# Stick-breaking units spread among the softmax units of block 1's attention, and head squares of block 2 moved to ScalarE

## The chip, the cores and the metric

The kernel runs on one core of one Trainium2 chip. The metric is the device time of one execution in microseconds (us); the time before is the median of three runs, 1567.66 us (1566.31 to 1568.97). Engines: PE is TensorE, ACT is ScalarE, DVE is VectorE, POOL is GpSimd, SP is the queue that loads the weights.

## The reference

Two blocks of two layers each, on 256 tokens of 1024 features, all in float32. Block 1, a layer:

```
h = rmsnorm(x, norm_mix);  proj = h @ w_in            # q, k, v of 24 heads of 64, and 3 x 1024 gate columns
o_a = dilated_mixture(q, k, v)       # 4 slots, each 3 heads of different dilation in one softmax
o_b = moba_attention(q, k, v)        # 6 heads, causal softmax
o_c = stick_breaking_attention(q, k, v)   # 6 heads, no softmax:
    z = q k^T * scale;  log_1m = log_sigmoid(-z) (0 where not causal)
    a = exp(log_sigmoid(z) + exclusive suffix sum of log_1m);  o = a v
merged = gates[0] * (o_a @ w_out_a) + gates[1] * (o_b @ w_out_b) + gates[2] * (o_c @ w_out_c)
x = x + merged @ w_o;  x = x + relu(rmsnorm(x) @ w_up)^2 @ w_down
```

Block 2 takes x and a context of 256 tokens. Each layer projects the modulated norm of both (512 rows), and every query and key head gets an RMS norm of its own:

```
def rms_norm(x, g): return x * rsqrt(mean(x * x, axis=-1) + EPS) * g      # over the 64 features of a head
q = apply_rope(rms_norm(heads(aq, 8), q_norm));  k = apply_rope(rms_norm(heads(ak, 2), k_norm))
```

Layer 0 has a global attention and a Hyena branch, layer 1 a windowed and a neighbourhood attention.

## The kernel before, in words

**Precision and staging.** Every large product is made of three fp32r passes (`product`, L617 to L619): high by high, and the two cross terms. Weights arrive in `raw` by SP, ACT rounds each quarter (128x1024) to `w_high` (L1343), and DVE subtracts it to `w_low` (L1756). There are four slots for split quarters, so a quarter is rounded when the product that used the one four before it has ended. The class `Splits` puts these roundings in ACT's and DVE's streams: `splits.due(key)` issues each rounding whose slot is free by the time PE reaches `key`. `copy_out`, which ACT uses to empty a bank, calls it first.

**Block 1's attention.** `units_of_block1` lists 26 units: 8 of kind A (four slots, two query tiles each), 12 of kind B (six heads, two tiles) and 6 of kind C, one per stick-breaking head. Before, all C stand last, as units 20 to 25. All three engines walk this list in step; for unit u PE runs `scores(u)`, `second(u-1)`, three or four steps of the gates' projection (`advance(filler, ...)`: three for A, four for B and C, a step being the three passes of one k and one tile) and `values(u-2)`. The 96 filler steps are six slabs of 16. The banks of a slab close when PE is in units 5, 9, 13, 17, 21 and 25, and ACT copies the two banks out at the end of the unit in which they close (`copy_gate`, L1447 and L1451, four instructions). In the next units it does a logarithm step (L1458, L1460) and an exponent step (L1466) for each. Three banks serve the gates.

- A softmax unit: scores on PE (L801, L806), mask and maximum on DVE (L1926 to L1942), exponential on ACT (L1379), transposes on PE (L832), copy on ACT (L1350), values on PE (L857), scaled copy on ACT (L1434).
- A C unit: scores on PE (L811, L812), mask on DVE (L1921), three instructions on ACT (L1478, L1480, L1482), then DVE (L1960, L1963: `stick_summed`), the suffix sums on PE (L822 to L824), DVE (L1947), an exponential on ACT (L1417: `stick_weights`), values on PE (L845 to L847), copy on ACT (L1429).

In ACT's stream a unit begins with `take_second(u-1)`, then the roundings that are due, then its exponential or its three C instructions, then `take_values(u-2)`, an exponent step, a logarithm step, and the gate copies. After the last unit PE waits until every `o` bank is empty and transposes the heads' outputs (L881); ACT and DVE split these (L1502, L1979), and the output projection starts (L617).

**Block 2's head norms.** `heads_norm` on DVE waits until ACT has emptied the banks, squares the heads tile by tile (L2098), sums the squares (L2100), and after ACT's Ln and Exp refines and multiplies (L2105 to L2118), with roundings' subtractions in between. PE transposes the normed heads (L1019) and starts the attention. The norms are (layer, j): (0, 0) and (1, 3) of 4 tiles x 8 heads, (0, 1) and (1, 1) of 4 tiles x 2 heads, (1, 0) and (1, 2) of 2 tiles x 8 heads. POOL meanwhile adds masks to the relative biases (L2541), and splits the last weights.

Of the kernel before, what the change touches and what calls it, by code (L numbers as in the profile page):

```python
# [26 lines left out]
ACT = mybir.ActivationFunctionType  # L27
# [115 lines left out]
def units_of_block1():  # L143

    soft = [("A", s, t) for s in range(N_A) for t in range(TILES)]
    soft += [("B", b, t) for b in range(N_B) for t in range(TILES)]
    return soft + [("C", c, 0) for c in range(N_C)]
# [64 lines left out]
def two_blocks(nc, A, C, out):  # L212
    ctx = ExitStack()
    with ctx:
# [61 lines left out]
        work = arena[:, 0:2048]  # L276
        ada_rows = arena[:, 2560:3072]
# [238 lines left out]
        def bank(*key):  # L516
            return banks[number[key][0]]
# [777 lines left out]
        def _(act):  # L1295
# [51 lines left out]
            def copy_out(dst, src, *key, scale=1.0):  # L1347
                splits.due(*key)
                act.wait_ge(*filled(*key))
                run(A_(dst, src, ACT.Copy, scale=scale), emptied(*key))  # L1350
# [197 lines left out]

            def heads_rsqrt(l, j, n):
                act.wait_ge(*heads_squared.at(l, j))  # L1550
                run(A_(nstat[:, 1, 0:n], nstat[:, 0, 0:n], ACT.Ln, bias=eps_col[:, 0:1], scale=1.0 / DH))
                run.settle()
                run(A_(nstat[:, 2, 0:n], nstat[:, 1, 0:n], ACT.Exp, scale=-0.5), heads_guess.by(l, j))
# [71 lines left out]
            for t in (2, 3, 0, 1):  # L1625
                copy_out(q2[:, t, :], bank("in2", 0, 0, t)[:, :], "in2", 0, 0, t)
            splits.due("in2", 0, 0, 1, ahead=1)
            heads_rsqrt(0, 0, T4 * QH)
            for t in range(T4):
                copy_out(kv2[:, t, :], bank("in2", 0, 1, t)[:, 0:256], "in2", 0, 1, t)  # L1630
# [60 lines left out]
            for t in (2, 3, 0, 1):  # L1691
                copy_out(nk[:, t, :], bank("in2", 1, 3, t)[:, :], "in2", 1, 3, t)
            splits.due("in2", 1, 3, 1, ahead=1)
            heads_rsqrt(1, 3, T4 * QH)
            for t in range(T4):
                copy_out(kv3[:, t, :], bank("in2", 1, 1, t)[:, 0:256], "in2", 1, 1, t)
# [23 lines left out]
        def _(dve):  # L1720
# [362 lines left out]
            def heads_norm(l, j, x, tiles, heads, g, rope, dup, ready, dues=()):  # L2083
# [12 lines left out]
                sq = work[:, 0:n * DH].rearrange("p (t h d) -> p t h d", t=tiles, h=heads)  # L2096
                for t in range(tiles):
                    run(V.tensor_tensor(sq[:, t], x3[:, t], x3[:, t], ALU.mult))  # L2098
                run.settle()
                run(V.tensor_reduce(nstat[:, 0, 0:n], work[:, 0:n * DH].rearrange("p (a d) -> p a d", d=DH), AX_X, ALU.add),  # L2100
                    heads_squared.by(l, j))
# [538 lines left out]
```

## Time and profile before

| what | value |
|---|---|
| median of 3 runs | 1567.66 us |
| profiled execution, its own time | 1568.89 us |
| its span | 1567.1 us |
| PE busy | 1496.2 us, 95% |
| DVE busy | 975.9 us, 62% |
| ACT busy | 773.7 us, 49% |
| POOL busy | 93.8 us, 6% |
| mean granted TensorE clock | 0.984 of 2.4 GHz |

The profiled execution took 1.23 us more than the median of the runs, and 1.8 us of it lie outside its span. The busy time of PE counts overlapping matmuls once; what is left, 71 us, is time in which PE stood. The timeline gives for each instruction its start, its duration, and in brackets how long its engine had stood before it and for whom. Matmul records overlap: the work that a group takes is read from one start to the next.

### The profile page before, as it was taken

Reading aid. Unit: us, or ns where it says so; the run is one execution under the profiler, and the core shown is the slowest. Engines: PE = TensorE matmul, PEld = TensorE weight load, DVE = VectorE, ACT = ScalarE, POOL = GpSimd, SP = SyncE. Lnnn points to the kernel's source line nnn. Section 1 sums busy time; section 2 is a strip of 40 time slices with the busy share of each in tenths; the row PEclk is TensorE's granted clock in tenths of the full one; section 3 lists DMA queues with packets and bytes.
Section 4 is the critical chain, followed back from the end, with each engine's and each line's share of the span. In section 5 each row is a group of like instructions: output and inputs, shape, how many; then the busy total and the mean of one; then the engine's idle time right before and its main releaser. Section 6 shows DMA issues by size and latency. Waiting matters only on the chain.

```text
span 1567.1 us, 21532 instructions
## 1 busy us (share of the span) xinstructions
PE 1496.2 (95%) x8288; PEld 1201.6 (77%) x8288; DVE 975.9 (62%) x1759; ACT 773.7 (49%) x1301; POOL 93.8 (6%) x142
## 2 busy tenths in 40 slices
PE   7999998999999999998999999989999999989987
PEld 6887776799887787877789978767775458777866
DVE  4553456766544554455757665685579863688865
ACT  5445785455444445777355554335443102434752
POOL 6050000000000000000000000000000000032210
PEclk9999999999999999999999999999998999999989
DMA  8781334697555754242779555452221001353100
GB/s 277 255 186 64 134 108 169 207 254 203 195 184 177 277 188 135 81 135 96 227 224 245 191 185 164 128 132 64 78 85 55 13 1 54 95 156 108 55 28 28
DMA packets 183412, 220.95 MB, mean 141 GB/s; under 512 B 6587, under 2 KB 103397, under 8 KB 183312
## 3 DMA queue, kind: packets, MB, share of 16 engines
q1 hardware_dynamic: 179088, 211.65, 42.7%
q0 software_dynamic: 3184, 7.93, 2.6%
q8 instruction: 67, 1.10, 0.3%
q14 instruction: 33, 0.27, 0.1%
q10 hardware_dynamic: 1040, 0.00, 0.0%
HBM read 216.55 MB, written 3.01 MB: 140 GB/s over the span
## 4 chain that ended last, share of the span: by engine, by line
PE 71%; DVE 18%; ACT 7%; issue 3%; DMA 0%; DVEq 0%; ACTq 0%; SPq 0%
PE bank L617 19%; PE bank L619 19%; PE bank L618 19%; DVE w_low L1756 3%; ACT w_high L1343 2%; DVE arena L2158 2%; PE bank L857 1%; PE bank L1092 1%; PE bank L801 1%; PE bank L1055 1%; PE bank L698 1%; PE bank L832 1%; PE bank L634 1%; PE bank L1068 1%; DVE arena L2112 1%
## 5 line engine op out<-in xcount | busy, mean ns | idle before, releaser
L1756 DVE TENSOR_TENSOR w_low<-raw,w_high 128x1024 fp32r<-128x1024 f32 x344 | 415.0, 1213 | 339.2 <-ACT w_high L1343 333.8
L1343 ACT ACTIVATE w_high<-raw 128x1024 fp32r<-128x1024 f32 x352 | 366.4, 1046 | 335.4 <-PE bank L619 283.8
L617 PE MATMUL bank<-w_high,acts_r 128*128 128x512 f32 (+1 forms) x848 | 340.1, 401 | 14.7 <-DVE w_low L1756 7.0
L619 PE MATMUL bank<-w_high,acts_r 128*128 128x512 f32 (+1 forms) x848 | 330.9, 390 | 0.0
L618 PE MATMUL bank<-w_low,acts_r 128*128 128x512 f32 (+1 forms) x848 | 330.8, 390 | 0.0
L617 PE MATMUL bank<-acts_r,w_high 128*128 128x256 f32 (+1 forms) x736 | 230.2, 313 | 3.5 <-DVE arena L2176 2.4
L618 PE MATMUL bank<-acts_r,w_high 128*128 128x256 f32 (+1 forms) x736 | 226.6, 308 | 0.0
L619 PE MATMUL bank<-acts_r,w_low 128*128 128x256 f32 (+1 forms) x736 | 226.3, 307 | 0.0
L617 PEld LDWEIGHTS bank<-w_high,acts_r 128*128 128x128 f32 x848 | 160.9, 190 | 57.0 <-DVE w_low L1756 8.9
L619 PEld LDWEIGHTS bank<-w_high,acts_r 128*128 128x128 f32 x848 | 160.0, 189 | 36.7
L618 PEld LDWEIGHTS bank<-w_low,acts_r 128*128 128x128 f32 x848 | 160.5, 189 | 32.1
L617 PEld LDWEIGHTS bank<-acts_r,w_high 128*128 128x128 f32 x736 | 140.1, 190 | 12.5 <-issue 3.1
L619 PEld LDWEIGHTS bank<-acts_r,w_low 128*128 128x128 f32 x736 | 139.8, 190 | 7.4
L618 PEld LDWEIGHTS bank<-acts_r,w_high 128*128 128x128 f32 x736 | 140.0, 190 | 6.6
L617 PE MATMUL bank<-w_high,hidden_r 128*128 128x512 f32 (+1 forms) x304 | 118.7, 390 | 0.0
L619 PE MATMUL bank<-w_high,hidden_r 128*128 128x512 f32 (+1 forms) x304 | 118.2, 389 | 0.0
L618 PE MATMUL bank<-w_low,hidden_r 128*128 128x512 f32 (+1 forms) x304 | 118.2, 389 | 0.0
L617 PEld LDWEIGHTS bank<-w_high,hidden_r 128*128 128x128 f32 x304 | 57.0, 187 | 13.6 <-issue 0.8
L619 PEld LDWEIGHTS bank<-w_high,hidden_r 128*128 128x128 f32 x304 | 57.0, 187 | 13.2
L618 PEld LDWEIGHTS bank<-w_low,hidden_r 128*128 128x128 f32 x304 | 57.0, 188 | 12.9
L1350 ACT ACTIVATE arena<-bank 128x512 f32<-128x512 f32 (+3 forms) x98 | 45.3, 483 | 39.2 <-PE bank L832 15.3
L1597 ACT ACTIVATE arena<-bank 128x512 f32<-128x512 f32 (+1 forms) x64 | 31.6, 543 | 30.1 <-PE bank L1068 29.8
(313 smaller groups left out, 1816.4 us busy)
## 6 DMA issues: line engine op xcount, KB each, us to landing
raw<-in_w_in SPq DMA_DIRECT2D x69, 1024.0 KB, 5.2
raw<-in_w_up SPq DMA_DIRECT2D x64, 512.0 KB, 6.9
raw<-in_w_down SPq DMA_DIRECT2D x32, 1024.0 KB, 4.9
raw<-in_w_ada SPq DMA_DIRECT2D x24, 1024.0 KB, 6.8
raw<-in_w_in SPq DMA_DIRECT2D x34, 512.0 KB, 5.1
raw<-in_w_o SPq DMA_DIRECT2D x8, 1024.0 KB, 7.3
raw<-in_w_out SPq DMA_DIRECT2D x8, 1024.0 KB, 5.0
raw<-in_w_out_c SPq DMA_DIRECT2D x4, 768.0 KB, 5.2
```

Of the source, the lines that this page charges most:

```text
L617: mm(o, lh, rh, start=start, stop=False)
L618: mm(o, lh, rl, start=False, stop=False)
L619: return mm(o, ll, rh, start=False, stop=stop)
L634: ins = mm(o[:, c:c + P], X[:, x0 + t, k * P:(k + 1) * P], scales[:, t, 0:P], start=True, stop=True)
L698: ins = mm(o[32 * j:32 * (j + 1), :], cond[:, 4 * h + j, :], w[:, j, :], start=h == 0, stop=h == 1)
L801: ins = mm(o[:, c:c + span], head(0, hd, q), head(1, hd, slice(0, span)), start=True, stop=True)
L832: ins = tr(o[:, (b - b0) * P:(b - b0 + 1) * P], S[:, u % 2, b * P:(b + 1) * P], ident[:, :])
L1343: run(A_(high, src, ACT.Copy), (high_ready, n + 1))
L1350: run(A_(dst, src, ACT.Copy, scale=scale), emptied(*key))
L1597: run(A_(PT2[:, u % 2, 0:n], bank("p", 2 + l, u, 0)[:, 0:n], ACT.Copy), emptied("p", 2 + l, u, 0))
L1756: run(V.tensor_tensor(low, src, high.bitcast(F32), ALU.subtract), split_done(n))
L2158: run(V.reciprocal(g, g))
```

## The change

The list of block 1 now puts one C unit before every third softmax unit: A A C A, A A C A, A A C B, B B C B, B B C B, B B C B, B B. The C units are 2, 6, 10, 14, 18 and 22; the filler still gives three steps in A and four in B and C. In block 2, ACT squares the heads of four norms, (0, 0), (0, 1), (1, 3) and (1, 1), from the bank, behind the copy of each bank and before the bank is marked empty; DVE begins these norms with the sum.

```diff
     soft = [("A", s, t) for s in range(N_A) for t in range(TILES)]
     soft += [("B", b, t) for b in range(N_B) for t in range(TILES)]
-    return soft + [("C", c, 0) for c in range(N_C)]
+    every = len(soft) // N_C
+    units = []
+    for c in range(N_C):
+        units += soft[c * every:(c + 1) * every - 1] + [("C", c, 0), soft[(c + 1) * every - 1]]
+    return units + soft[N_C * every:]
...
+        squares_at = {(0, 0): 0, (1, 3): 0, (0, 1): 2048, (1, 1): 2048}
...
+            def copy_and_square(dst, l, j, t, n):
+
+                key = ("in2", l, j, t)
+                splits.due(*key)
+                act.wait_ge(*filled(*key))
+                run(A_(dst, bank(*key)[:, 0:n], ACT.Copy))
+                w = n if j in (0, 3) else KVH * DH
+                at = squares_at[l, j] + t * w
+                run(A_(arena[:, at:at + w], bank(*key)[:, 0:w], ACT.Square), emptied(*key))
...
             for t in (2, 3, 0, 1):
-                copy_out(q2[:, t, :], bank("in2", 0, 0, t)[:, :], "in2", 0, 0, t)
+                copy_and_square(q2[:, t, :], 0, 0, t, GW)
...
             for t in range(T4):
-                copy_out(kv2[:, t, :], bank("in2", 0, 1, t)[:, 0:256], "in2", 0, 1, t)
+                copy_and_square(kv2[:, t, :], 0, 1, t, 2 * KVH * DH)
...
             for t in (2, 3, 0, 1):
-                copy_out(nk[:, t, :], bank("in2", 1, 3, t)[:, :], "in2", 1, 3, t)
+                copy_and_square(nk[:, t, :], 1, 3, t, GW)
...
             for t in range(T4):
-                copy_out(kv3[:, t, :], bank("in2", 1, 1, t)[:, 0:256], "in2", 1, 1, t)
+                copy_and_square(kv3[:, t, :], 1, 1, t, 2 * KVH * DH)
...
-                sq = work[:, 0:n * DH].rearrange("p (t h d) -> p t h d", t=tiles, h=heads)
-                for t in range(tiles):
-                    run(V.tensor_tensor(sq[:, t], x3[:, t], x3[:, t], ALU.mult))
-                run.settle()
-                run(V.tensor_reduce(nstat[:, 0, 0:n], work[:, 0:n * DH].rearrange("p (a d) -> p a d", d=DH), AX_X, ALU.add),
-                    heads_squared.by(l, j))
+                at = squares_at.get((l, j), 0)
+                sq = arena[:, at:at + n * DH]
+                if (l, j) not in squares_at:
+                    for t in range(tiles):
+                        run(V.tensor_tensor(sq.rearrange("p (t h d) -> p t h d", t=tiles, h=heads)[:, t], x3[:, t], x3[:, t], ALU.mult))
+                    run.settle()
+                run(V.tensor_reduce(nstat[:, 0, 0:n], sq.rearrange("p (a d) -> p a d", d=DH), AX_X, ALU.add), heads_squared.by(l, j))
```

How the order of instructions moves, at three places.

ACT, layer 0 of block 1, around the end of the slab that closes in unit 13. Before: the exponent step, the four gate copies, then a rounding and unit 13's transposes, exponential of unit 14, a softmax unit.

```order
L1434 ACTIVATE arena<-bank,stat 128x64
L1466 ACTIVATE arena<-arena 128x512
L1447 ACTIVATE arena<-bank,nstat 128x512
L1451 ACTIVATE arena<-bank,nstat 128x512
L1447 ACTIVATE arena<-bank,nstat 128x512
L1451 ACTIVATE arena<-bank,nstat 128x512
L1343 ACTIVATE w_high<-raw 128x1024
L1350 ACTIVATE arena<-bank 128x256
L1379 ACTIVATE arena,stat<-arena,stat 128x128
```

In the changed kernel (its lines are 5 higher here) unit 14 is a C, and its three instructions stand behind the same six:

```order
L1439 ACTIVATE arena<-bank,stat 128x64
L1471 ACTIVATE arena<-arena 128x512
L1452 ACTIVATE arena<-bank,nstat 128x512
L1456 ACTIVATE arena<-bank,nstat 128x512
L1452 ACTIVATE arena<-bank,nstat 128x512
L1456 ACTIVATE arena<-bank,nstat 128x512
L1348 ACTIVATE w_high<-raw 128x1024
L1355 ACTIVATE arena<-bank 128x128
L1483 ACTIVATE arena<-arena 128x384
L1485 ACTIVATE arena<-arena 128x384
L1487 ACTIVATE arena<-arena,eps_col 128x384
```

What moved is the C unit: three ACT instructions stand where one exponential stood.

ACT, the end of block 1's attention in layer 0, from the gate copies of the last slab to the high parts of the transposed outputs. Before, the last unit is a C and one rounding stands behind all of it:

```order
L1447 ACTIVATE arena<-bank,nstat 128x512
L1451 ACTIVATE arena<-bank,nstat 128x512
L1417 ACTIVATE arena<-arena 128x384
L1429 ACTIVATE arena<-bank 128x2x64
L1458 ACTIVATE arena<-arena 128x512
L1460 ACTIVATE arena<-arena,eps_col 128x512
L1429 ACTIVATE arena<-bank 128x2x64
L1458 ACTIVATE arena<-arena 128x512
L1460 ACTIVATE arena<-arena,eps_col 128x512
L1466 ACTIVATE arena<-arena 128x512 x2
L1343 ACTIVATE w_high<-raw 128x1024
L1502 ACTIVATE acts_r<-bank 128x512 x4
```

In the changed kernel the last unit is a B, and the rounding stands between the gate copies and its bank's copy:

```order
L1452 ACTIVATE arena<-bank,nstat 128x512
L1456 ACTIVATE arena<-bank,nstat 128x512
L1348 ACTIVATE w_high<-raw 128x1024
L1355 ACTIVATE arena<-bank 128x256
L1439 ACTIVATE arena<-bank,stat 128x64
L1463 ACTIVATE arena<-arena 128x512
L1465 ACTIVATE arena<-arena,eps_col 128x512
L1439 ACTIVATE arena<-bank,stat 128x64
L1463 ACTIVATE arena<-arena 128x512
L1465 ACTIVATE arena<-arena,eps_col 128x512
L1471 ACTIVATE arena<-arena 128x512 x2
L1507 ACTIVATE acts_r<-bank 128x512 x4
```

What moved is the rounding, by nine instructions, because `copy_out` asks for what is due and the C unit's path does not.

DVE, block 2 layer 1, norm (1, 3). Before, and (second fence) in the changed kernel:

```order
L1756 TENSOR_TENSOR w_low<-raw,w_high 128x512 x4
L2098 TENSOR_TENSOR arena<-arena 128x512 x4
L2100 TENSOR_REDUCE nstat<-arena 128x32
L1756 TENSOR_TENSOR w_low<-raw,w_high 128x1024
L2105 TENSOR_SCALAR nstat<-nstat 128x32
```

```order
L1771 TENSOR_TENSOR w_low<-raw,w_high 128x512 x4
L2117 TENSOR_REDUCE nstat<-arena 128x32
L1771 TENSOR_TENSOR w_low<-raw,w_high 128x1024
L2121 TENSOR_SCALAR nstat<-nstat 128x32
L1741 TENSOR_TENSOR nstat<-nstat 128x32
```

The four squares are gone from DVE's stream, and nothing else of it moved.

## Rows read from the trace of the kernel before

**Rows 1.** The chain that ended last, by engine, share of the span

```profile
PE 71%; DVE 18%; ACT 7%; issue 3%; DMA 0%; DVEq 0%; ACTq 0%; SPq 0%
```

**Rows 2.** Who waited for whom on PE: us in total, times, longest

```profile
PE bank L822 <- DVE arena L1963: 7.9, 12, 1.1
...
PE bank L617 <- ACT arena L1451: 2.4, 4, 0.6
...
PE bank L1019 <- DVE arena L2143: 1.6, 1, 1.6
```

**Rows 3.** Timeline, PE, layer 1: start us, us, line, operation, count, idle before

```profile
668.39 0.55 PE L857 MATMUL bank<-arena 128*128 128x64 f32 x4
...
694.05 0.70 PE L811 MATMUL bank<-arena 64*128 64x256 f32 x2
...
699.53 0.70 PE L822 MATMUL bank<-arena 128*128 128x256 f32 x2 [0.39 <-DVE arena L1963]
...
727.13 0.33 PE L845 MATMUL bank<-arena 128*128 128x64 f32 x2
...
729.02 0.70 PE L822 MATMUL bank<-arena 128*128 128x256 f32 x2 [1.12 <-DVE arena L1963]
...
731.72 0.43 PE L845 MATMUL bank<-arena 128*128 128x64 f32 x2 [0.94 <-ACT arena L1417]
...
733.52 3.53 PE L881 MATMUL bank<-ident,arena 128*128 128x128 f32 x16 [0.92 <-ACT arena L1429]
...
738.83 0.50 PE L617 MATMUL bank<-w_high,acts_r 128*128 128x512 f32 x1
```

**Rows 4.** Timeline, ACT, layer 1

```profile
668.98 0.31 ACT L1434 ACTIVATE arena<-bank,stat 128x64 f32<-128x64 f32 x1 [1.64 <-PE bank L857]
...
669.71 0.68 ACT L1447 ACTIVATE arena<-bank,nstat 128x512 f32<-128x512 f32 x1
...
671.99 1.08 ACT L1343 ACTIVATE w_high<-raw 128x1024 fp32r<-128x1024 f32 x1
...
672.94 0.41 ACT L1350 ACTIVATE arena<-bank 128x256 f32<-128x256 f32 x1
...
696.86 0.51 ACT L1478 ACTIVATE arena<-arena 128x384 f32<-128x384 f32 x1
```

**Rows 5.** Timeline, DVE, layer 1

```profile
698.92 0.56 DVE L1963 SCALAR_TENSOR_TENSOR arena<-arena 128x384 f32<-128x384 f32 x1
```

**Rows 6.** Timeline, ACT, DVE and PE, block 2 layer 0

```profile
1011.86 1.30 ACT L1350 ACTIVATE arena<-bank 128x512 f32<-128x512 f32 x2 [1.41 <-PE bank L619]
...
1014.74 2.49 DVE L2098 TENSOR_TENSOR arena<-arena 128x512 f32<-128x512 f32 x4
...
1035.96 0.89 DVE L2098 TENSOR_TENSOR arena<-arena 128x128 f32<-128x128 f32 x4
...
1025.22 0.47 PE L617 MATMUL bank<-acts_r,w_high 128*128 128x512 f32 x1 [1.05 <-DVE w_low L1756]
```

**Rows 7.** Timeline, POOL and DVE, block 2 layer 1

```profile
1376.16 14.41 POOL L2541 TENSOR_TENSOR arena<-arena 128x256 f32<-128x256 f32 x16 [10.22 <-DMA arena<-const_mask_n]
...
1378.06 4.65 DVE L2098 TENSOR_TENSOR arena<-arena 128x512 f32<-128x512 f32 x4
...
1382.74 2.29 DVE L2100 TENSOR_REDUCE nstat<-arena 128x32 f32<-128x2048 f32 x1
...
1390.87 2.50 DVE L2112 TENSOR_TENSOR arena<-arena,nstat 128x512 f32<-128x512 f32 x4
...
1393.40 1.23 DVE L1756 TENSOR_TENSOR w_low<-raw,w_high 128x1024 fp32r<-128x1024 f32 x1
```

**Rows 8.** Timeline, PE, start of block 2's second attention

```profile
1442.56 1.02 PE L1055 MATMUL bank<-acts_r,hidden_r 64*128 64x512 f32 x6 [2.33 <-DVE hidden_r L2188]
```

**Rows 9.** Timeline, PE, start of block 1's first attention

```profile
121.10 0.47 PE L617 MATMUL bank<-w_high,acts_r 128*128 128x512 f32 x1 [1.64 <-ACT arena L1350]
```

**Rows 10.** Stretches of 10 us: busy of each engine, PEclk, DMA share, GB/s

```profile
120.00:130.00 10.00, 8.90 (x25) 6.38 (x26) 2.98 (x11) 3.74 (x9) 0.00 (x0) 0.66 0.32 105
```

## The prediction

> **What bounds the kernel now.** I read the chain that ended last first: 71% of it is PE, 18% DVE, 7% ACT [rows 1]. So the time is PE's work, which the change leaves alone, plus the places where PE stands; the question is only which stands go and which come. The list of PE's waits comes next [rows 2]. In block 1 PE waits 12 times, 7.9 us, for L1963, the stick sum of a C unit, and 4 times, 2.4 us, for a gate bank that ACT has not emptied. That is six C waits and two bank waits in each layer. In block 2 it waits 1.6 us at L1019 for the end of DVE's head norm. Then the timelines, for what a C unit's chain is made of, and for what ends a stage.
>
> **Block 1, the C waits.** In layer 1 unit 20, a C, begins its scores at 694.05 and reaches its second product at 699.53, of which 0.39 is waiting [rows 3]: PE has 5.1 us of other work to cover a C unit's chain. The units of a C and a B differ by some tenths there, so I use 5.1 for a C among B units too (an A neighbour gives more). The chain itself goes through ACT. The change puts C units 10, 14, 18 and 22 behind the ends of gate slabs (units 9, 13, 17, 21), so ACT comes to them in this order, timed from the C's scores: 0.1 us until the value bank is full, value copy and exponent step 0.73 (668.98 to 669.71), four gate copies 2.28 (669.71 to 671.99), a rounding 0.95 (671.99 to 672.94), the softmax unit's bank copy 0.15 to 0.26 [rows 4], then the three C instructions and DVE's sum, 2.4 (696.86 to the end of L1963 at 699.48 is 2.6, of which DVE was 0.2 late) [rows 4, 5]. Sum 6.6 to 6.7. PE needs 5.1, plus about 0.4 that it waits for a gate bank on the way, 5.5. **Stand: 1.2 us** at units 10, 14 and 22. At unit 18 both neighbours on PE are short (one-tile B units) and the copied bank is the longer one: 1.7. Unit 6 stands among A units of long PE work and no slab ends just ahead: 0. Unit 2: 0.2. The softmax unit next to a C does not hide it: it is ACT's backlog of gate copies, not the neighbouring C, that makes the chain long.
>
> Worked the same way, the waits before come out some 0.1 long each, so of 5.5 for the six C units I keep 5.0 a layer. The bank wait stays at three slab ends, 0.4 each, where it was two of 0.6: 1.2 both times. Before, the C waits other than the last cost 7.9/2 - 1.12 = 2.8 a layer [rows 2, 3]; the last belongs to the tail. **Ahead of the filler's end: +2.2 us a layer.**
>
> **Block 1, the tail.** From the end of the filler (727.13) to the outputs' transposes (733.52) are 6.39 us, and the next stage starts at 738.83, 11.7 after the filler's end [rows 3]. ACT sets this: gate copies, last bank, logarithm and exponent steps, rounding. PE's own work in the 6.39 is what is left without the waits 1.12, 0.94 and 0.92: 3.4 us, that of four C pieces (the values of three, the sums of one), less 0.4 of ends that no wait shows: 3.0. In the changed kernel B pieces stand there, 1.4 in all by their starts (a one of two tiles is recorded with 0.55 [rows 3]). So 1.6 us of C work move out of the shadow of ACT's tail to a place where PE is the bound: **+1.6 a layer**. Inside the tail PE will stand long in front of the last unit's values: value wait 0.5, exponent step and copy 0.73, gate copies 2.28, now also the rounding 0.95 and the bank copy 0.26, together 4.8 [rows 4] against 0.9 of PE work: 3.9 to 4.0 us. It costs little by itself, since ACT's stream behind it is no longer than before: transposes at 6.7 instead of 6.4, and as the rounding is then done, 0.9 less behind them. **-0.6 a layer.**
>
> Block 1: 2.2 + 1.6 - 0.6 = 3.2, and by the chain with the waits followed unit by unit 3.0; I take 3.05 a layer, **+6.1**.
>
> **The clock.** After a wait of 1.64 us [rows 9] the stretch from 120 to 130 has a granted clock of 0.66 [rows 10]: of 10 us some 6.8 at 1.2 GHz instead of 2.4. The transposes of layer 1 at 733.52, behind waits of 1.12, 0.94 and 0.92, take 3.53 us for 16 [rows 3], the lower level too. The new stand of 4.0 us will bring it as surely; the transposes then take their 3.5 us again, and most of it lies beside ACT's last steps: **+0.3 a layer, +0.6.** The stands of 1.2 and 1.7 have no such cover; that is a rival.
>
> **Block 2, layer 0.** Removed from DVE: four squares of norm (0, 0), 2.49 us, and four of (0, 1), 0.89 [rows 6]. Added on ACT: a square behind each copy, at the copy's pace, 0.6 (two copies of 512 columns take 1.30 [rows 6]). The last two banks are thus empty 1.2 later, and DVE, which waits for them, starts 1.2 later and has 2.5 less: -1.3. (0, 1) follows without a wait, its squares on ACT being done long before: -0.9. PE reaches the feature groups without the wait of 1.05 [rows 6], and then waits for DVE at L1019 about 0.5 instead of 1.6 [rows 2]; DVE's end sets both times: **-2.2**. ACT's roundings behind the squares are late by 1.2 and not missed: PE has three split quarters in hand.
>
> **Block 2, layer 1.** The squares of (1, 3) took 4.65 us there instead of 2.5, because they stood beside POOL's 16 additions from 1376.16 to 1390.57; the sum of squares, in the same stretch, took 2.29, undisturbed [rows 7]. Without them the sum ends 3.5 earlier: squares 4.65 and start 1.2 later. But now the small steps and the multiplication L2112 (2.50 when it stood behind POOL [rows 7]) fall into POOL's stretch, at the squares' 1.16 each: two of the four, and a late small step. The subtraction that PE waits for (1393.40 [rows 7]) comes 1.4 earlier, not 3.5. (1, 1) adds 0.9. PE stands 2.33 for DVE at 1442.56 [rows 8], so DVE's gain counts whole: **-2.35**.
>
> The Trainium skill says (SBUF — State Buffer, "Who interferes with whom") that a VectorE instruction with two SBUF inputs and a GpSimd instruction that reads SBUF exclude each other for a whole instruction, and that tensor_reduce never contends. The trace agrees: 4.65 against 2.49 for the squares, 2.29 for the sum. By it POOL's additions, no longer held up by the squares, would end some 2.5 us sooner, L2112 would be free again, and the time would be that of the third rival.
>
> **Sum.** +6.1 + 0.6 - 2.2 - 2.35 = +2.1 us. On the profiled execution's 1568.89 that gives 1571.0; the median of the runs is 1.23 lower, so for the median **1569.8 us**. A measurement of this kernel tells some 0.2%, 3.1 us, from no change. My forecast is no change that can be told, on the slow side.
>
> **Rivals.**
> - **The clock falls inside the attention (slower, 28%).** The stand of 1.7 us at unit 18 is as long as the one of 1.64 that was followed by the lower clock [rows 9, 10]. Behind it PE is the bound, so each fall of 3.4 to 6.8 us costs half of that, 1.7 to 3.4, once or twice a layer: +3 to +7 in two layers, 1573 to 1576. It decides as soon as one of the stands among B units is followed by 1.2 GHz. For it: the length of the stand. Against: the waits of 1.05 to 1.12 were not each followed by a fall.
> - **Block 2 gives less (slower or same, 10%).** If ACT's squares hold the banks so long that PE or DVE waits for ACT in turn, only the small norms' 1.8 us and a little are won: 1568 + 6.7 - 3 = 1571.5. Against: ACT stands 5.9 us behind its last copy anyway, which the removed chain covers.
> - **POOL ends sooner (same, 12%).** POOL's 16 additions take 14.41 us, and while the squares stood beside them these took 4.65 instead of 2.49 [rows 6, 7]. If POOL was held up as long as DVE was, it ends 2.2 to 2.5 us sooner without them, L2112 runs alone in 2.50, and this norm gives 1.2 more: +0.9 in all, 1568.6. For it: the sum of squares beside the same additions was not slowed, so two kinds of instruction stood in each other's way there, and the changed kernel has one of them less.
> - **The C units are hidden (faster, 9%).** If ACT comes to a C's instructions ahead of the gate copies, or a softmax neighbour covers the chain, the waits of 5.0 a layer are not there: 2.2 becomes -2.8, block 1 comes to 3.05 - 5.0 = -1.95 a layer, and the sum to -3.9 + 0.6 - 2.2 - 2.35 = -7.85, 1559.8; with or without the bank waits (2.4 in two layers) and the longer tail, 1555 to 1563. For it: before, a C waits for the C ahead of it (the wait grew from 0.39 at the first to 1.12 at the last), and the change takes that apart. Against: the same rows put the gate copies, 2.3 us, ahead of four of the six.
>
> **The numbers.** Forecast 41% (1567.5 to 1572, mostly under the bound of 1570.8). Faster by over 0.2%: 0.11, nearly all from the last rival. Within: 0.45 (two thirds of the forecast, the POOL case, a part of block 2's). Slower: 0.44 (a third of the forecast, the clock, the rest). Range 1565.5 to 1575.5: it leaves out the hidden C units below, and above the case of a fall of the longer kind twice in each layer.
>
> **What would show it.** In the profile after: waits of PE for the stick sum of about 1.2 us at four units a layer, 5 us in all where it was 3.9; a wait of about 4 us for the copy of the last unit's bank, in each layer; the transposes of the heads' outputs again at 3.5 us; the wait at the head transposes of block 2's layer 0 down to about 0.5; norm (1, 3)'s sum ending at 3.5 us less after its last copy, and L2112 longer than 2.5. What would make it wrong: no waits at the C units; a granted clock under 0.9 in the stretches of the B units ahead of the tail; or norms of block 2 that give less than 1 us each pair, to be read from the starts of L1019 against those of the products ahead of them.

## The result and the profile after

The changed kernel took 1575.86 us (median of 4 runs, 1574.84 to 1576.59), the kernel before 1567.05 us beside it (4 runs, 1566.31 to 1568.97): a ratio of 1.0054, 95% interval 1.0036 to 1.0071. It is slower by 8.8 us, where the forecast said +2.1 with a range that ended at 1575.5; the time is one of those given for the rival in which the clock falls inside the attention (1573 to 1576), but only about half of what the forecast missed is that rival's mechanism, as shown below. A repeat of the same kernel gave 1575.96 against 1567.54, ratio 1.0049 (1.0034 to 1.0064).

First the waits of PE in the changed kernel, to be read against [rows 2]. Columns: who waited for whom, us in total, times, longest. The changed kernel's line numbers are 5 higher in block 1 and 15 or 16 higher further on.

```profile
PE bank L1097 <- DVE arena L2257: 11.1, 11, 4.3
PE bank L827 <- DVE arena L1978: 11.0, 10, 1.7
PE bank L862 <- ACT arena L1355: 8.1, 2, 4.1
...
PE bank L622 <- DVE w_low L1771: 6.1, 3, 3.4
...
PE bank L622 <- ACT arena L1456: 1.4, 6, 0.3
```

The stick sum (L1978) now costs 11.0 us in 10 waits instead of 7.9 in 12; a new wait of 4.06 stands once in each layer; the wait for a gate bank (L1456) is down to 1.4 us; and the wait at the head transposes of block 2's layer 0 (1.6 us) is no longer in the list. The first row belongs to block 2's second attention and was 11.2 before; the fourth, PE waiting for DVE's subtraction of a weight, was 8.1 in 4 waits. Next the timeline of PE in layer 1, where unit 18's second product and the tail stand (columns as in [rows 3]):

```profile
664.33 0.70 PE L827 MATMUL bank<-arena 128*128 128x256 f32 x2 [1.22 <-DVE arena L1978]
...
684.24 0.70 PE L827 MATMUL bank<-arena 128*128 128x256 f32 x2 [1.17 <-DVE arena L1978]
...
703.36 1.11 PE L827 MATMUL bank<-arena 128*128 128x256 f32 x2 [1.70 <-DVE arena L1978]
...
723.97 0.70 PE L827 MATMUL bank<-arena 128*128 128x256 f32 x2 [1.17 <-DVE arena L1978]
...
740.81 0.91 PE L862 MATMUL bank<-arena 128*128 128x64 f32 x4 [4.06 <-ACT arena L1355]
742.68 3.65 PE L886 MATMUL bank<-ident,arena 128*128 128x128 f32 x16 [0.96 <-ACT arena L1439]
...
748.90 0.50 PE L622 MATMUL bank<-w_high,acts_r 128*128 128x512 f32 x1
```

The waits are those that were forecast, to a tenth: 1.2 at units 10, 14 and 22, 1.7 at 18, 4.06 for the last bank. But the product behind the stand of 1.70 takes 1.11 instead of 0.70. It runs at the lower clock, as the stretches show (columns as in [rows 10]; the second is the tail):

```profile
700.00:710.00 10.00, 8.30 (x35) 6.53 (x33) 4.86 (x10) 6.54 (x14) 0.00 (x0) 0.83 0.31 105
735.00:750.00 15.00, 9.98 (x54) 6.89 (x53) 6.15 (x11) 10.35 (x20) 0.00 (x0) 0.77 0.32 113
```

ACT's stream ahead of that product is the queue of the forecast: four gate copies, a rounding, the bank copy, and only then the C unit's three instructions.

```profile
697.40 0.68 ACT L1452 ACTIVATE arena<-bank,nstat 128x512 f32<-128x512 f32 x1
...
699.11 0.71 ACT L1456 ACTIVATE arena<-bank,nstat 128x512 f32<-128x512 f32 x1
699.67 1.08 ACT L1348 ACTIVATE w_high<-raw 128x1024 fp32r<-128x1024 f32 x1
700.62 0.41 ACT L1355 ACTIVATE arena<-bank 128x256 f32<-128x256 f32 x1
700.88 0.55 ACT L1483 ACTIVATE arena<-arena 128x384 f32<-128x384 f32 x1
```

**Where the time went.** I read the starts of the same PE instructions in both traces and took the differences stage by stage. The kernel before was profiled a second time in the experiments, and the first profile holds a stretch at the lower clock that the second does not (attention of layer 0: 131.50 us in the first, 128.37 in the second, all other stages of block 1 within 0.1). Against the second:

| stage, PE start to PE start | before | changed |
|---|---|---|
| block 1 layer 0: first scores to output transposes | 128.37 | +5.74 |
| output transposes to the transposes of the merged heads | 23.54 | -0.05 |
| block 1 layer 1: first scores to output transposes | 127.76 | +5.83 |
| output transposes to the transposes of the merged heads | 23.64 | +0.87 |
| block 2 layer 0: up to the head transposes | 139.91 | -3.14 |
| block 2 layer 1: projections and norms | 103.95 | -1.85 |
| block 2 layer 1: attention to the end | 118.15 | +1.43 |
| the rest | 887.8 | -0.6 |

Block 1 lost 12.4 us, block 2's norms gained 5.0, and the end of the program, which the change does not touch, lost 1.4. The stages add up to 8.2; the spans of these two executions differ by 8.8.

The loss at the end comes at one place. Up to 61 us into that stage the changed kernel has lost nothing (0.03 us). Then it runs for 3.4 us at the lower clock, on work that the other does at the full clock (columns as in [rows 10]; first the changed kernel, then the second profile of the kernel before, from the same instruction on):

```profile
1505.00:1515.00 10.00, 7.86 (x63) 6.85 (x62) 7.21 (x33) 4.75 (x11) 0.00 (x0) 0.83 0.30 104
```

```profile
1497.60:1507.60 10.00, 7.62 (x82) 6.70 (x81) 7.58 (x35) 6.33 (x15) 0.00 (x0) 1.00 0.28 104
```

### The profile page after: what moved, and what is told of

It is laid out like the page before. It is cut to its first block, busy times and chain, and to the rows that moved or that the text cites. A ratio compares the mean times of both kernels' runs of the same rounds, so it can differ in the third digit from the quotient of the medians.

```text
span 1574.8 us, 21580 instructions
## 1 busy us (share of the span) xinstructions
PE 1501.0 (95%) x8288; PEld 1205.7 (77%) x8288; DVE 970.1 (62%) x1743; ACT 779.5 (49%) x1317; POOL 93.4 (6%) x142
## 4 chain that ended last, share of the span: by engine, by line
PE 74%; DVE 15%; ACT 6%; issue 2%; DMA 1%; DVEq 0%; SPq 0%; ACTq 0%
PE bank L622 20%; PE bank L624 20%; PE bank L623 20%; DVE w_low L1771 2%; DVE arena L2174 2%; ACT w_high L1348 2%; PE bank L1097 1%; PE bank L862 1%; PE bank L703 1%; PE bank L1060 1%; PE bank L806 1%; PE bank L639 1%; PE bank L837 1%; DMA raw<-in_w_up 1%; ACT arena L1452 1%
## 5 line engine op out<-in xcount | busy, mean ns | idle before, releaser
L1348 ACT ACTIVATE w_high<-raw 128x1024 fp32r<-128x1024 f32 x352 | 367.3, 1048 | 345.1 <-PE bank L624 292.5
L624 PEld LDWEIGHTS bank<-w_high,hidden_r 128*128 128x128 f32 x304 | 57.0, 187 | 13.2
L1355 ACT ACTIVATE arena<-bank 128x512 f32<-128x512 f32 (+3 forms) x82 | 38.1, 486 | 30.5 <-PE bank L1209 13.6
```

What stands on the lines that cost most here:

```text
L624: return mm(o, ll, rh, start=False, stop=stop)
L1348: run(A_(high, src, ACT.Copy), (high_ready, n + 1))
```

## The experiments

Each ran on one chip beside the kernel before. The clock is the mean over the runs of the granted clock; that of the kernel before is 0.985 or 0.986 in each set, and of the changed kernel 0.980.

| kernel | median us | beside it, before | ratio (95%) | clock |
|---|---|---|---|---|
| units only | 1580.92 | 1567.73 | 1.0087 (1.0074, 1.0100) | 0.979 |
| squares only | 1560.45 | 1567.73 | 0.9953 (0.9941, 0.9965) | 0.987 |
| C units at 2, 6, 9, 13, 17, 21 | 1562.42 | 1567.73 | 0.9966 (0.9954, 0.9979) | 0.982 |
| C units at 2, 6, 13, 17, 21, 25 | 1555.05 | 1567.73 | 0.9924 (0.9911, 0.9937) | 0.986 |
| C units at 2, 6, 10, 14, 18, 25 | 1563.90 | 1567.73 | 0.9977 (0.9964, 0.9990) | 0.986 |
| last rounding behind | 1571.56 | 1567.73 | 1.0025 (1.0015, 1.0035) | 0.982 |
| masks later | 1558.10 | 1567.73 | 0.9936 (0.9924, 0.9948) | 0.987 |
| before again | 1567.76 | 1567.73 | 1.0000 (0.9991, 1.0009) | 0.985 |
| change again | 1575.96 | 1567.54 | 1.0049 (1.0034, 1.0064) | 0.980 |
| C unit 18 at 17 | 1569.99 | 1567.54 | 1.0015 (1.0006, 1.0023) | 0.981 |
| tail stand filled | 1568.50 | 1567.54 | 1.0007 (0.9998, 1.0016) | 0.988 |
| C stands filled | 1570.84 | 1567.54 | 1.0022 (1.0013, 1.0030) | 0.984 |
| both filled | 1568.53 | 1567.67 | 1.0007 (0.9998, 1.0016) | 0.987 |
| best places, filled | 1557.23 | 1567.67 | 0.9926 (0.9914, 0.9938) | 0.987 |

### The two parts apart

Units only is the kernel before with the new list of units; squares only is the changed kernel with the old list:

```diff
-    every = len(soft) // N_C
...
-    return units + soft[N_C * every:]
+    return soft + [("C", c, 0) for c in range(N_C)]
```

> Only the new order of the units; block 2's squares stay on DVE. Theory A (the change is the sum of its two parts as its trace shows them, the gain of block 2 being 4.6 us): 1575.9 + 4.6 = 1580.5, and PE waits in each layer of about 1.2 at units 10, 14 and 22, 1.7 at 18, 4.0 for the last unit's bank. Theory B (my forecast's term for block 1, 6.7 us, was right, and the excess of the changed kernel comes from block 2's part or from nowhere in particular): 1573 to 1574.

> Only the squares on ACT; the units in the old order. Theory A: 1567.0 - 4.6 = 1562.4. Theory B (block 2's part gives back in its second attention the 2.1 us that the trace of the change shows there): 1564.5 or more. In the trace: no wait of 1.0 at the product ahead of the head transposes of layer 0, the multiplication behind norm (1, 3)'s sum at 4.6 us instead of 2.5.

Measured 1580.9 (+13.2) and 1560.5 (-7.3). Theory A holds in sign and size for the units: the block 1 part alone costs twice the 6.7 us of my term. The squares gave 2.7 more than the traces of the change had shown. Part of that is the clock: in the profile of the squares alone block 2 is 6.2 shorter than before and not 5.0, and the stretch at the lower clock in layer 1's norms lasts 3.4 us and not 6.8. The two parts sum to +5.9 where the change has +8.4 to +8.8; each of these figures is uncertain by some 2 us, so this does not show that they fail to add.

### Where a C unit stands against the gate copies

```diff
-    every = len(soft) // N_C
...
-        units += soft[c * every:(c + 1) * every - 1] + [("C", c, 0), soft[(c + 1) * every - 1]]
-    return units + soft[N_C * every:]
+    every = iter(soft)
+    return [("C", (2, 6, 9, 13, 17, 21).index(u), 0) if u in (2, 6, 9, 13, 17, 21) else next(every) for u in range(len(soft) + N_C)]
```

> The changed kernel with its last four C units one unit earlier, 9, 13, 17 and 21: into the units in which a gate slab closes, so that ACT comes to their three instructions ahead of the four gate copies. Theory A (the waits at the C units are ACT's backlog of gate copies): they fall from 1.2, 1.2, 1.7, 1.2 to under 0.8 each, the waits for a gate bank go, no fall of the clock behind unit 17 or 18, 4.7 us less in each layer ahead of the outputs' transposes and 1.6 more of the clock: 1575.9 - 9.5 - 3.2 = 1563. Theory B (a C among softmax units waits for its own chain whatever stands on ACT): same waits, 1575.9 within 2 us.

Measured 1562.4, theory A. ACT's timeline of this kernel around unit 13, where a slab closes: the same instructions, with the C unit's three ahead of the gate copies.

```profile
185.41 0.52 ACT L1480 ACTIVATE arena<-arena 128x384 f32<-128x384 f32 x1
185.97 0.53 ACT L1482 ACTIVATE arena<-arena 128x384 f32<-128x384 f32 x1
186.53 0.62 ACT L1484 ACTIVATE arena<-arena,eps_col 128x384 f32<-128x384 f32 x1
...
188.39 0.68 ACT L1449 ACTIVATE arena<-bank,nstat 128x512 f32<-128x512 f32 x1
```

PE's second product of that unit waits 0.70:

```profile
188.74 0.70 PE L824 MATMUL bank<-arena 128*128 128x256 f32 x2 [0.70 <-DVE arena L1975]
```

In layer 0 PE then waits 0.70, 0.49 and 0.70 at units 13, 17 and 21, nothing at 9, and for no gate bank, where the changed kernel waited 1.22, 1.17, 1.71 and 1.17. Four units, one place in the list, 13.4 us; in the two profiles 12.7 us of it lie in the two attentions, 3.2 of them the clock that did not fall behind the late unit.

The next kernel moves only the C unit with the longest wait, from 18 to 17.

> The changed kernel with one C unit moved, from place 18 to 17, ahead of the gate copies. Theory A (the stand of 1.7 us costs itself and the clock behind it): wait 0.5 instead of 1.7 and no wait for a gate bank, 1.6 less in each layer, and 0 to 1.6 more of the clock: 1575.9 - 3.2 to 6.4 = 1569.5 to 1572.7. Theory B (C units anywhere in the region of the gate slabs cost the same sum, the wait moves to the next one): 1575 to 1577.

Measured 1570.0, theory A: one unit in each layer, one place, 6.0 us below the repeat of the change. The attention of layer 1 is 3.2 us shorter than in the change, 1.6 of waiting and 1.6 of the clock.

### The last unit

Here the C units stand at 2, 6, 10, 14, 18 and 25, and in the second kernel at 2, 6, 13, 17, 21 and 25.

> The changed kernel with its last C unit moved from place 22 to the end, so that one of the four late C units goes and the tail is the old one. Theory A (the softmax unit as the last costs by itself: PE's C work has moved out of the shadow of ACT's tail): waits of 1.2, 1.2 and 1.7 stay at units 10, 14 and 18, that of 4.0 goes; 2.9 us less in each layer to the outputs' transposes, some 0.9 of it given back behind them: 1575.9 - 2 x 2.0 to 2 x 2.9 = 1570 to 1572. Theory B (only the places against the gate copies count): one wait of 1.2 less in each layer, 1573.5.

Measured 1563.9, 12.0 less than the change, twice what theory A gave. Up to the output transposes its profile has 3.0 less in layer 0 and 4.6 less in layer 1. In layer 0 the clock fell behind unit 18 in both kernels, so 3.0 is the wait of one C unit and the C work that goes back beside ACT's tail; the other 1.6 in layer 1 is a fall of the clock behind unit 18 that did not come. Both runs of transposes take 1.94 here instead of 3.4 to 3.65, so the clock did not fall in the tail either:

```profile
735.42 1.94 PE L883 MATMUL bank<-ident,arena 128*128 128x128 f32 x16 [0.99 <-ACT arena L1431]
```

> The changed kernel with the C units at 2, 6, 13, 17, 21 and 25: ahead of the gate copies as in the run before it, and the last of them the last unit again. Theory A (two costs of the change in block 1: where a C stands against the gate copies, and a softmax unit as the last): the tail is that of the kernel before (waits of 1.1, 1.2 and 1.0 instead of 4.0 and 1.0), both costs gone, and C work still spread: 1567.0 - 2 x 2.9 - 4.6 = 1556.6. Theory B (block 1 is bound by ACT's tail however the units stand): block 1 as before, 1562.4.

Measured 1555.1, theory A (forecast 1556.6). Each attention is 2.9 us shorter than before, in both layers. This version beats both kernels: 12.7 us below the kernel before, 20.8 below the change. It keeps the idea of the change, C units among softmax units, and differs in where they stand.

The next kernel is the changed one, but the rounding that the last unit's copy pulls ahead (L1348) stands behind that unit's work again:

```diff
-                        copy_out(PT[:, u % 2, b0 * P:b0 * P + n], bank("p", l, u, b0 // 4)[:, 0:n], "p", l, u, b0 // 4)
+                        if u == len(U) - 1:
+                            act.wait_ge(*filled("p", l, u, b0 // 4))
+                            run(A_(PT[:, u % 2, b0 * P:b0 * P + n], bank("p", l, u, b0 // 4)[:, 0:n], ACT.Copy), emptied("p", l, u, b0 // 4))
+                        else:
+                            copy_out(PT[:, u % 2, b0 * P:b0 * P + n], bank("p", l, u, b0 // 4)[:, 0:n], "p", l, u, b0 // 4)
```

> The changed kernel with the rounding that the last softmax unit's copy pulled ahead put back behind the unit's work, where it stood in the kernel before. Both theories: the wait for the last bank is 3.1 instead of 4.06, the outputs' transposes start 0.95 earlier. Theory A (my forecast: the rounding has to be done anyway, ahead or behind): the next stage starts at the same time, 1575.9 within 0.5. Theory B (the next stage is bound by PE at the lower clock, and the rounding behind is covered): 1 us a layer less, 1574.

Measured 1571.6, 4.3 less, which neither theory had. In its profile the mechanism is that of theory A: the wait is 3.12, the transposes start 1.0 earlier than in the kernel with the C stands filled (the one to compare with, as the clock did not fall there either), and the stage behind them takes 1.3 longer in layer 0 and 0.3 in layer 1 than in the change. But the clock did not fall behind unit 18 in either layer, which is worth up to 3.2 of the 4.3. Its 11 runs spread from 1567.4 at a mean clock of 0.986 to 1575.8 at 0.978. So the difference goes with the clock; whether the shorter stand brings it was not tested alone.

### The clock by itself

In these kernels every wait for ACT and DVE stays. PE opens the bank first, transposes the identity into it a fixed number of times and waits only then; the real work overwrites the result.

```diff
+                    o = open_bank("o", l, u, among=ATTENTION_BANKS)
+                    if u == len(U) - 1:
+                        for _ in range(30):
+                            tr(o[:, 0:P], ident[:, :], ident[:, :])
                     for b0 in range(0, blocks, 4):
                         pe.wait_ge(*emptied("p", l, u, b0 // 4))
-                    o = open_bank("o", l, u, among=ATTENTION_BANKS)
```

> The changed kernel with 30 transposes of the identity (3.4 us at the higher clock, their result is overwritten) on PE in the stand of 4.06 us ahead of the last unit's values, in each layer: the same waiting for ACT, but PE is not idle in it. Theory A (that stand brings the lower clock, and the work behind it pays): the outputs' transposes take 1.9 instead of 3.6, the next stage starts 5.2 behind them or less instead of 6.2, mean clock up by 0.003 to 0.004, 0.5 to 1.5 us less in each layer: 1573 to 1575. Theory B (the clock falls anyway, or its price is covered by ACT and DVE): 1575.9 within 0.7.

Measured 1568.5, 7.4 less, where theory A had 1 to 3. The transposes take 1.94 in layer 0. The stages behind them are 1.0 shorter in each layer than in the change, 2.0 in all. The rest lies elsewhere. Of the 9.5 us by which this profile is shorter than that of the change, 3.1 are in the attentions, where the clock did not fall behind unit 18, and 4.1 in block 2's layer 1. In layer 0 unit 18 comes before the first filling, so the fall that is missing there is not the filling's doing in that execution. What the filling is shown to be worth is the 2.0; why the other falls are missing too is open. The fill in layer 1 first, then the stretch of layer 0's tail, whose granted clock is 0.76 in the changed kernel:

```profile
732.36 3.45 PE L859 MATMUL bank<-ident 128*128 128x128 f32 x30
736.58 0.66 PE L865 MATMUL bank<-arena 128*128 128x64 f32 x4 [0.78 <-ACT arena L1358]
```

```profile
246.00:260.00 14.00, 11.56 (x81) 8.78 (x80) 7.41 (x13) 10.65 (x20) 0.00 (x0) 1.00 0.23 73
```

> The changed kernel with transposes of the identity in the stands ahead of the late C units' second product, 8 (0.9 us) at units 10, 14 and 22, 12 (1.36 us) at unit 18: every unit starts when it did, but PE is not idle. Theory A (falls of the clock behind these stands are part of the change's loss): no low stretch in the attentions ahead of the tail, mean clock up by 0.001 to 0.002, 1 to 3 us less, 1573 to 1575. Theory B (they are no part of it, the loss is the waiting alone): 1575.9 within 0.7.

Here the fills of 8, 8, 12 and 8 stand in `second`, ahead of the wait for `stick_summed`. Measured 1570.8, 5.1 less, somewhat over theory A. Its granted clock is 1.00 from the first scores of each attention to the stand ahead of the last unit's values. Both attentions take 4.25 and 4.29 us more than before instead of 5.74 and 5.83: with the clock held, what is left is the 4.2 of waiting and moved work. The stretch from 700 to 710 in this kernel:

```profile
700.00:710.00 10.00, 9.75 (x54) 7.82 (x53) 5.39 (x13) 8.11 (x17) 0.00 (x0) 1.00 0.30 107
```

> The changed kernel with both fillings: transposes of the identity in the stands ahead of the late C units' second product and in the stand ahead of the last unit's values. All waits for ACT and DVE as in the change. Theory A (what each filling took off is the clock behind its own stands): both take off their own, 1575.9 - 7.4 - 5.1 = 1563.4, mean clock 0.989 or more, attention 4.2 longer than before in each layer still. Theory B (each filling took off the same thing, falls later in the program that depend on what the clock did earlier): no more than the larger of the two, 1568.5 within 1.

Measured 1568.5, theory B: no better than the tail's filling alone. Block 1 behaves as theory A had it. Its attentions are 4.27 and 4.30 over those of before, as with the C stands filled, and behind them it takes 1.0 less in layer 0 and the same in layer 1. Block 1 in all is 7.6 over before, where the change is 12.4 over: 4.8 us are the clock in block 1. The tail's filling alone has 7.3 in its profile, since no fall came behind a C unit in that execution. The larger part of what the fillings took off beyond this lies in block 2, whose instructions are the same in all of these kernels. There the stretches at the lower clock differ: the stage from the last attention to the end takes 1.4 more than before in the change and in its repeat, 1.1 less with the tail filled, 0.2 less with the C stands filled, 2.5 less with both. Why they fall otherwise there is open.

> The changed kernel, unchanged, for a second profile and five more granted clocks. Theory A (the last part of its loss is the clock, and falls behind stands of 1.7 us come in some executions and not in others): mean clock 0.980 to 0.981 again, 1574 to 1577, attention of a layer 134 us where the clock fell behind unit 18 and 132 where it did not. Theory B (a fall behind unit 18 is sure): 134 in both layers again.

Measured 1576.0. Layer 0 took 4.18 more than before and layer 1 5.82: a fall behind unit 18 in one layer of two, theory A. Over the profiles of all kernels that have the unfilled stand of 1.7 at unit 18 (six, so twelve stands), the clock fell behind five. Of forty unfilled stands of 1.2 it fell behind two. In or behind the twelve unfilled stands of 4.06 it fell every time, for 6.8 or 10.2 us. The old tail, with three stands of 0.9 to 1.1 close together, is no safe place either: the clock fell there nine times in twelve, for 3.4 us in six of the nine. So the length of one stand does not decide alone.

> The kernel before, unchanged, to see what a second profile and the granted clocks of five executions show. Theory A (the stretch of 6.8 us at the lower clock at the start of block 1's first attention came by chance with that execution): not there in this profile, attention 1 of layer 0 takes 128.3 instead of 131.5 us, and low stretches differ from execution to execution by some 1.7 us of time each. Theory B (it belongs to the kernel before, and the change takes it away): 131.5 again.

Measured 1567.8, theory A: 128.37. The stretch in [rows 10] came by chance with that execution; the same wait of 1.64 stands there in every profile of this study, and the low stretch behind it in one.

### Two that gave nothing

```diff
             pool.wait_ge(bias_loaded, BIASES * 16)
+            pool.wait_ge(*heads_ready.at(1, 3))
```

> The kernel with the C units at 2, 6, 13, 17, 21 and 25 and squares on ACT, and POOL's 16 mask additions held until DVE has finished norm (1, 3). Theory A (what is left of PE's stand of 3.7 us there is DVE slowed by POOL): the four small steps fall from 0.67 to about 0.19 each, the multiplication from 4.6 to 2.5, the stand from 3.7 to under 0.5; POOL's additions then stand beside norm (1, 1), whose multiplications have slack: 3.2 less, 1551.9. Theory B (it is only moved: norm (1, 1) and the subtractions behind are late in its place): PE stands as long behind it, 1555 within 1.

Measured 1558.1, 3.0 more than without the wait: theory B and more. Norm (1, 3) did go as theory A said, and norm (1, 1) paid. DVE's timeline of this kernel, the multiplication of (1, 3) and the two of (1, 1):

```profile
1375.12 2.50 DVE L2125 TENSOR_TENSOR arena<-arena,nstat 128x512 f32<-128x512 f32 x4
...
1386.03 3.03 DVE L2125 TENSOR_TENSOR arena<-arena,nstat 128x128 f32<-128x128 f32 x4
...
1390.65 3.06 DVE L2131 TENSOR_TENSOR arena<-arena,head_gain 128x128 f32<-128x128 f32 x4
```

The small ones take 3.03 instead of 0.90: beside POOL's additions DVE's short instructions started 0.70 to 0.76 us apart, whether of 8 columns or of 128. PE stands 2.04, 1.18 and 0.79 for the subtractions queued behind them, and 3.80 at the start of the attention, where the kernel without the added wait stands 3.71 in the norms, 0.73 at the start of the attention and 1.59 soon after.

The last kernel fills the stands of the best one.

> The kernel with the C units at 2, 6, 13, 17, 21 and 25 and squares on ACT, with 3, 5, 3 and 8 transposes of the identity ahead of the second product of the last four C units and 7 ahead of the last unit's values. Theory A (the low stretches at the end of its attentions, 3.4 us each, cost what those of the change do): 1 to 3 us less than 1555.1, 1552 to 1554. Theory B (ACT's and DVE's tail covers them): 1555 within 0.7.

Measured 1557.2 beside 1567.7, a ratio of 0.9926 against 0.9924 without fillings: theory B, as far as five runs from 1552.3 to 1557.8 can tell. In its profile no stretch of block 1's attentions or tails is at the lower clock any more, and yet the attentions are no shorter (2.88 and 2.83 under those of before, 2.95 and 2.93 without fillings). So the falls of 3.4 us at the end of these attentions cost nothing that the starts of PE's instructions show.

## Why the prediction was wrong

**Block 1, the C waits: right.** The steps named four units with a chain of ACT's backlog and gave 1.2, 1.2, 1.7 and 1.2; measured 1.22, 1.17, 1.70 and 1.17, with 0.26 at unit 2 and nothing at 6. That is 5.5 a layer, where the sum kept 5.0; the bank waits in turn came to 0.27 each and not 0.4. Moving the same units one place cut them to 0.5 to 0.7, so the cause is shown and not only the size.

**Block 1, the tail up to the transposes: right.** The forecast was +1.6 of moved work and a stand of 3.9 to 4.0; it is 4.06. With the 2.2 of the waits and the 0.3 by which the tail was to last longer (6.7 instead of 6.4) the transposes should start 4.1 us later. With the C stands filled they do, by 4.25 and 4.29.

**The tail behind the transposes, -0.6: right at the higher clock only.** I credited the rounding done ahead with 0.9 us there. With the tail filled, layer 0 has -1.0, and layer 1, in which a low stretch of 3.4 us came with the transposes, -0.1. In the change itself, at the lower clock, the stage measured -0.05 and +0.87: PE's own transposes (3.4 to 3.65 us instead of 1.94) and the products behind them then take the time in which PE otherwise stands for DVE, 0.96 us in layer 0 of the first profile before.

**The clock: the step that failed most.** My sum held +0.3 a layer for it, on the ground that the lower clock would lie beside ACT's last steps; the runs show 1.6 a layer behind unit 18 and 1.0 a layer behind the transposes. The rival with 28% described the first of these: the stand of 1.7 at unit 18 is followed by 1.2 GHz, in both layers in the first profile, for 1.6 us each; its price was right and its chance too low. The sign that I had named for it, a granted clock under 0.9 among the B units, is there with 0.83. But that the time fell on the rival's 1573 to 1576 is half luck: with its 3.2 us alone the forecast would be 1573.0, and the other 2.9 were in no rival. The argument against it, that waits of about 1.1 were not each followed by a fall, spoke of the shorter stands only. For the longer one [rows 9, 10] did show a fall, though by the repeat that one was rare. And the stand of 4.06 did not cost 0.3 a layer: its filling took 1.0 a layer off the stages just behind.

**Block 2: close in sum, in part by luck.** Forecast -4.55, measured -5.0 in the traces. In layer 0 the gain was 3.14 instead of 2.2: both of PE's stands, 1.05 and 1.63, are gone, because the sum starts 1.76 sooner after the last copies (5.41 us before, 3.65 now) and not 1.3; a square adds about 0.5 to the copies' pace and not 0.6. In layer 1 the subtraction came 16.9 us after the start of the copies instead of 18.3, the 1.4 of the forecast, but by other terms. The sum of squares ended 4.1 sooner and not 3.5, and all four multiplications fell beside POOL's additions, 2.1 us more, and not two of them, 1.1. The forecast's own terms, 3.5 less 1.1 less 0.5 for a small step, give 1.9 and not the 1.4 that it wrote. DVE's timeline there:

```profile
1394.82 4.58 DVE L2128 TENSOR_TENSOR arena<-arena,nstat 128x512 f32<-128x512 f32 x4
1399.43 1.23 DVE L1771 TENSOR_TENSOR w_low<-raw,w_high 128x1024 fp32r<-128x1024 f32 x1
```

The multiplication takes 4.58 instead of 2.50 because POOL's additions still stand beside it, so the rival in which POOL ends in time did not come about. POOL did get shorter, but by 0.46 us, 13.95 against 14.41 [rows 7], and not by the 2.2 to 2.5 of that rival: the multiplications stood beside it in the squares' place. Before, five of the 16 additions took 1.18 us, now four; one took 1.72 both times, and the others 0.74. It also started 2.4 us after the first copy instead of 1.1: its masks landed later.

```profile
1384.90 13.95 POOL L2557 TENSOR_TENSOR arena<-arena 128x256 f32<-128x256 f32 x16 [11.55 <-DMA arena<-const_mask_n]
```

The Trainium skill (SBUF — State Buffer, "Who interferes with whom") has the rule for the direction: two-input VectorE instructions contend with GpSimd's reads and tensor_reduce does not. The held masks agree with it, since DVE's two-input instructions slowed down wherever POOL's additions were put and its reduction did not (0.67 for the small one beside them, 0.68 alone). DVE's one-input steps (L2121) slowed down as well, 0.71 instead of 0.17. What each collision costs is for the rows to say.

The stage's -1.85 also holds more of the lower clock than before: 6.8 us of it behind that subtraction instead of 3.4. Of the profiles with the squares on ACT and norm (1, 3) as here, six have the 6.8 and are 1.7 to 2.2 shorter than before in this stage; three have 3.4 and are 3.2 to 3.5 shorter (in the last three it lies elsewhere). Read off these profiles, and not tested by itself: with as much of the lower clock as before, the squares would have given some 6.4 us and not 4.55, and the clock took 1.4 of it back.

**The end of the program, +1.4: not in the forecast.** It is one more stretch of 3.4 us at the lower clock, as the rows under the stage table show. No term or rival held a change in a part whose instructions stay the same, and why the clock falls there is open.

In sum, by the stages: +2.1 was forecast. To it come 3.2 for the falls behind unit 18, 2.0 for the tail behind the transposes, 0.5 of small differences in block 1, -0.45 for block 2, 1.4 at the end and -0.6 for the rest: 8.2. Of block 1's 12.4, 7.6 stay when every stand is filled, the waits and the moved work; 4.8 are the clock.

The failed step, then, is the term of the clock. The sum held +0.6 for it, all of it in the tail, and nothing for the stands of the C units. Block 1 alone shows 4.8, and that is the least, since with both stands filled layer 1's transposes still ran at the lower clock. A further 1.4 came at the end of the program, where the cause of the fall stays open.

## What to carry to other kernels

When work of one kind is spread among another, what counts is not the neighbour but what stands ahead of it in the busiest helper's queue: four units, each one place earlier in a list of 26, ahead of four gate copies instead of behind them, were worth 13.4 us here, the clock included. Price a stand of PE twice: once for its length and once for the clock behind it; the second price is a chance (here five falls in twelve stands of 1.7 us, twelve in twelve of 4 us), and filling the stand with idle transposes helps to find it, if the gain is read stage by stage: the total of one kernel also moves by falls elsewhere. And leave the unit whose own work covers the others' tail at the end, where a short last unit only waits.

## What the runs showed that I had not expected

- Work that does nothing made the kernel faster: 30 transposes of the identity in each layer, 7.4 us less, with the mean clock going from 0.980 to 0.988. Only 2.0 of it are shown to come from those stands.
- The stretches at the lower clock lasted 3.4, 6.8, 10.2 or 13.7 us in all sixteen profiles, but for the one behind the last products.
- A kernel's own runs differ by its clock: over the 111 runs of the experiments an execution with 0.001 less of mean clock took about 0.8 us more than others of its kernel (0.4 to 1.8, kernel by kernel).
- Low stretches in one part of the program went together with others in a part that runs the same instructions 800 us later. The repeat of the change had the same ones there as the first, which speaks against pure chance; what links them was not found.
